# A planner's clock for TensorE that counts changes of the used part of the array

## The reference, cut to what matters

```python
def first_block(x, p, ...):
    for l in range(DEPTH):
        mix = even_mixer(...) if l % 2 == 0 else odd_mixer(...)
        x = layer_norm(ALPHA * x + mix, ln1_g[l], ln1_b[l])
        hdn = jnp.square(jax.nn.relu(x @ ffn_w1[l]))
        x = layer_norm(ALPHA * x + hdn @ ffn_w2[l], ln2_g[l], ln2_b[l])
        e = rms_norm(p[l] @ ple_w_proj[l], ple_norm_g[l])
        x = x + jax.nn.sigmoid(x @ ple_w_gate[l]) * e
    return x
```

## Time and profile before

| | |
|---|---|
| median of 3 runs | 1855.76 us (1855.68 to 1857.1) |
| profiled execution, span from first to last instruction | 1854.1 us |
| PE busy | 1788.8 us, 96% |
| DVE busy | 1275.2 us, 69% |
| ACT busy | 990.7 us, 53% |
| mean granted clock of PE | 0.989 |

### The profile page before, as it was taken

One profiled execution on the slowest core, in us unless ns is written; L12 is line 12 of the kernel. 1 busy time (PEld: TensorE's weight loads), 2 busy tenths in 40 slices (PEclk: granted clock), 3 DMA queues, 4 the chain that ended last, 5 costly groups with the idle time before them and its releaser, 6 DMA issues. The chain is left out here.

```text
span 1854.1 us, 35690 instructions
## 1 busy us (share of the span) xinstructions
PE 1788.8 (96%) x14792; PEld 1663.2 (90%) x14792; DVE 1275.2 (69%) x2351; ACT 990.7 (53%) x1741; POOL 76.2 (4%) x78
## 2 busy tenths in 40 slices
PE   7999999999999999999889999999999999989997
PEld 6778899978888999999889988899999898679997
DVE  5566656568778755886766777765676867876665
ACT  4565545466556544654755655554455555644443
POOL 0000100020000200000100101000000000100000
PEclk9999999999999999999999999999999999989999
DMA  9797865676344555455454443455655543236663
GB/s 377 273 354 253 325 184 190 185 291 195 122 117 140 165 185 185 126 171 182 128 174 155 149 159 93 150 178 184 186 177 193 162 137 107 86 114 185 184 186 120
DMA packets 93825, 334.92 MB, mean 181 GB/s; under 512 B 10960, under 2 KB 12880, under 8 KB 93536
## 3 DMA queue, kind: packets, MB, share of 16 engines
q1 hardware_dynamic: 92016, 327.33, 54.1%
q0 software_dynamic: 1648, 5.31, 0.9%
HBM read 331.55 MB, written 1.05 MB: 179 GB/s over the span
## 5 line engine op out<-in xcount | busy, mean ns | idle before, releaser
L565 DVE TENSOR_TENSOR low<-ring,high 128x1024 fp32r<-128x1024 f32 x410 | 500.8, 1223 | 218.4 <-ACT high L557 209.0
L590 PE MATMUL bank<-XHx,high 128*128 128x256 f32 x2096 | 608.7, 290 | 21.9 <-DVE low L565 9.7
L591 PE MATMUL bank<-XLx,high 128*128 128x256 f32 x2096 | 592.2, 283 | 0.0
L592 PE MATMUL bank<-XHx,low 128*128 128x256 f32 x2096 | 591.0, 282 | 0.0
L557 ACT CAST high<-ring 128x1024 fp32r<-128x1024 f32 x410 | 428.6, 1045 | 276.0 <-PE bank L592 230.5
L590 PEld LDWEIGHTS bank<-XHx,high 128*128 128x128 f32 x2096 | 397.6, 190 | 41.3 <-issue 9.7
L591 PEld LDWEIGHTS bank<-XLx,high 128*128 128x128 f32 x2096 | 398.1, 190 | 1.5 <-issue 0.2
L592 PEld LDWEIGHTS bank<-XHx,low 128*128 128x128 f32 x2096 | 398.2, 190 | 0.0
L590 PE MATMUL bank<-XHc,high_side 128*128 128x256 f32 x608 | 180.9, 297 | 10.2 <-DVE low_side L565 8.1
L591 PE MATMUL bank<-XLc,high_side 128*128 128x256 f32 x608 | 172.0, 283 | 0.0
L592 PE MATMUL bank<-XHc,low_side 128*128 128x256 f32 x608 | 171.7, 282 | 0.0
(11 more groups left out here) (448 smaller groups left out, 3052.1 us busy)
## 6 DMA issues: line engine op xcount, KB each, us to landing
ring<-in_stream SPq DMA_DIRECT2D x410, 512.0 KB, 3.7
ring_side<-in_stream SPq DMA_DIRECT2D x110, 512.0 KB, 3.7
ring_mod<-in_stream SPq DMA_DIRECT2D x96, 512.0 KB, 8.0
x_nb<-in_rpb POOLq DMA_DIRECT2D x6, 256.0 KB, 3.1
x_late_NB<-in_rpb POOLq DMA_DIRECT2D x6, 256.0 KB, 3.1
Xx<-in_x SPq DMA_DIRECT2D x2, 512.0 KB, 5.8
Xc<-in_ctx SPq DMA_DIRECT2D x1, 1024.0 KB, 7.0
out<-y SPq DMA_DIRECT2D x8, 128.0 KB, 2.0
```

The source lines that it names most:

```text
L565: nc.vector.tensor_tensor(st.low[:, j % st.n_ring, :], st.ring[:, j % st.n_ring, :], st.high[:, j % st.n_split, :].bitcast(F32), ALU.subtr ...
L590: nc.tensor.matmul(out, wh, xh, start=(i == 0), stop=False)
L591: nc.tensor.matmul(out, wh, xl, start=False, stop=False)
L592: m = nc.tensor.matmul(out, wl, xh, start=False, stop=(c == ks[-1]))
```

## The change

TensorE's lane remembers which part of the array was used last (`rows_cols`). Every place that emits matmuls now first calls `T.shape(rows, cols)`, which adds 0.2 us to the clock when the part differs from the last one. A full product's pass is charged n / 2180 us, other matmuls n x passes / 2370 without the 0.006. The 64x64 pieces of GLA are charged 0.03 us, its state steps three passes instead of four, and the 0.45 us for each run of modulation tiles is dropped. Nothing else is changed: no instruction is added or removed, and the plans and ranks stay.

```diff
@@ class Lane
+        self.rows_cols = P, P
...
+    def shape(self, rows, cols):
+        if (rows, cols) != self.rows_cols:
+            self.clock += SHAPE_US
+            self.rows_cols = rows, cols
...
 def T_us(n, passes=1):
-    return max(n * passes / 2270.0, 0.06) + 0.006
+    return max(n * passes / 2370.0, 0.06)
+
+
+def pass_us(n):
+    return n / 2180.0
+
+
+SHAPE_US, QUARTER_US = 0.2, 0.03
...
@@ def products (and rows_product, in the same way)
+            T.shape(P, P)
...
-                m.then_inc(*T.tick(k.s_products, 3 * T_us(n), key, *used))
+                m.then_inc(*T.tick(k.s_products, 3 * pass_us(n), key, *used))
...
-                T.spend(3 * T_us(n))
+                T.spend(3 * pass_us(n))
...
@@ def tensor_modulations
+                T.shape(P, 32)
...
-                if c % MOD_BATCH == 0:
-                    T.spend(0.45)
...
+            T.shape(P, P)
...
@@ def tensor_scores
+            T.shape(HD, P)
...
@@ def tensor_values
+                T.shape(P, P // len(one))
...
@@ def tensor_gla
+        T.shape(32, P)
...
+            T.shape(HD, CH)
...
-                        T.spend(T_us(CH, 2))
+                        T.spend(QUARTER_US)
...
+            T.shape(CH, P)
...
-                *T.tick(k.s_states, T_us(P, 4), (tag(i), "step", n)))
+                *T.tick(k.s_states, T_us(P, 3), (tag(i), "step", n)))
...
+            T.shape(HD, HD)
...
-                T.spend(T_us(CH, 2))
+                T.spend(QUARTER_US)
```

More of the change, by code:

```diff
@@ L593, in products @@
             if c == ks[-1]:
-                m.then_inc(*T.tick(k.s_products, 3 * T_us(n), key, *used))
+                m.then_inc(*T.tick(k.s_products, 3 * pass_us(n), key, *used))
             elif used:
-                m.then_inc(*T.tick(st.s_used, 3 * T_us(n), *used))
+                m.then_inc(*T.tick(st.s_used, 3 * pass_us(n), *used))
             else:
-                T.spend(3 * T_us(n))
+                T.spend(3 * pass_us(n))
             yield None
@@ L633, in rows_product @@
             if c == DC - 1:
[L634 removed]
+                m.then_inc(*T.tick(k.s_products, 3 * pass_us(n), keys[i], *mine))
             elif mine:
[L636 removed]
+                m.then_inc(*T.tick(st.s_used, 3 * pass_us(n), *mine))
             else:
[L638 removed]
+                T.spend(3 * pass_us(n))
             yield None
@@ L1597, in tensor_hgrn @@
     k.bank_of[tag, "inner"] = b0
+    T.shape(P, CH)
     for i in range(2 * NQ):
@@ L1842, in tensor_gla @@
                     if c == CHUNKS - 1:
-                        m.then_inc(*T.tick(k.s_mixers, T_us(CH, 2), (tag(i), "inner scores", hh)))
+                        m.then_inc(*T.tick(k.s_mixers, QUARTER_US, (tag(i), "inner scores", hh)))
                     else:
-                        T.spend(T_us(CH, 2))
+                        T.spend(QUARTER_US)
             yield None
@@ L1869, in tensor_gla @@
         halves = [slice(hh * HD, (hh + 1) * HD) for hh in range(2)]
+        T.shape(P, HD)
         for tile in range(NQ):
```

## The result

| | before | changed |
|---|---|---|
| median | 1856.43 us (1855.68 to 1858.21) | 1867.22 us (1865.39 to 1868.23) |
| ratio, 95% interval | | 1.0065 [1.0049, 1.0081] |
| span of the profiled execution | 1854.1 us | 1866.9 us |

The account below looks back on a forecast made before the run. TensorE, busy 1788.8 of 1854.1 us, was taken as the bound, so order could move only idle time, lower-clock time and shape changes. 1855.8 - 5.6, all else nil, gave 1850.2 us; range 1839 to 1866.

Parts of the forecast that it names:

- The sum of the clock: TensorE's planner clock, order unchanged: -14.4 - 10.8 - 23.5 + 64.6 = +15.9 us over the kernel, about +4 by 902 us.
- the tie at 902: Layer norm near 902 us: the side tile's low part goes before the norm's steps on DVE, -5.6 us (uncertain from 0).
- The second term: All other reordered choices across the kernel: gains and losses cancel, taken as nil; change count bounded at 6.4 us either way.
- The slower rival: Side tiles due earlier cause a new PE wait during a norm: 8.8 us more, 1864.6 us; chance 0.24.
- the two-tile ring: Side tile buffer: each tile needs 8.0 us from the freeing of its place, so PE may wait during a norm.
- earlier due times: Side stream's plan, 840 to 1300 us: 0.5 tile more asked for at 902, 1.5 to 2 at the stretch's end.
- the prediction's own signs of being wrong: Whole kernel: a wait over 3 us at a new place, lower-clock stretches growing, or change count moving over a tenth.
- The other signs: Near 900 us: wait 2 us or less, no lower clock; around 960: wait 4 to 5 us; 1000 to 1300: side one to two tiles ahead.
- The ring's chain: Side tile at 962.88 us: load at 954.91 to PE's start takes 8.0 us, little shortened by rank; gain taken as 0.
- the rule about draining: Changing the tiling mode drains TensorE; each change is paid whether booked or not, so booking alone would gain nil.

Follow-up runs that it names:

- the two tried orders: Changed kernel with small moves of its charge, lag and plan constants, two sets chosen by replaying the orders: 1846.60 us (0.9951) and 1849.36 us (0.9964).
- side plan +1: Changed kernel with every time of the side stream's plan 1 us later (481, 841, 1301, 1531): 1857.61 us, ratio 1.0015 to the kernel before.

## Why the prediction was wrong

The sum of the clock held. The order moved almost everywhere, the number of changes of shape was 318 (323 before, forecast 290 to 355), and the single charges are what the rows show. PE's busy time rose by 7.0, at the very edge of the 7 us allowed; 5.7 of that is the lower clock.

The step that failed is the one from there to a time, in both of its terms. The first is the tie at 902, put at -5.6. It did not turn: the norm moved by 18 us, another side tile met it, and its low part came 4.4 us after its cast, as in the old order. PE's wait for a side tile (5.4 us) is gone there, but one of 4.3 us for the gate's first product stands at the same norm, with 6.8 us at the lower clock from 922.2 on. The second term is everything else, put at nothing ("the reshuffled ties gain here what they lose there"). With the first term at nothing, the second measured +10.8: new waits of PE and the clock after them, 5.8 and 5.7 us by the two profiles. A saving at one place of a list schedule can't be forecast with the rest of the order held fixed, since the order after it is another.

Is the second term zero in the mean? Of the nine kernels above in which charges or the plan were moved without trial (all but the two tried orders), eight are slower than the kernel before, by 0.15 to 1.2%, and one equals it. Six of the nine are the changed kernel and its neighbours, so they are no even sample. But none of them is faster: the kernel before is low in the spread, though not the lowest, as the tried orders show, and a move from it is likely up. Nothing in its profile says so directly, but the size of what the order can move was there to read: 65.3 us not busy and 20.4 at the lower clock, less the start and the norms.

The range failed by the same step. Its upper end allowed one new wait of 5.4 us with its echo in the clock (8.8 us, 1864.6, and 1.4 around it). There came seven of 1.9 to 4.7 us for the three that went, and the time was 1.2 us above the range. The slower rival had the sign, and its mechanism, the two-tile ring while a norm runs, made one of the seven waits (1492 us; 7.9 us from load to use, forecast 8.0). The wait of 3.1 at 1218 is for a side tile too; the other five are of other kinds. Its reason, earlier due times, is not borne out: with the side stream two tiles later the kernel is slower still, and with the plan 1 us later it is nearly back. Two of the prediction's own signs of being wrong were met: waits over 3 us stand at 925, 1218 and 1492, where there was none, and the stretches at the lower clock grew.

The other signs: the wait for a side tile in the c_hidden products around 960 was to stay at 4 to 5 us and is gone. The ring's chain is there, from a load at 956.91 to a low part that begins at 961.69, but PE has other work meanwhile; so another order can cover such a chain, which the prediction priced at no gain. No stretch at the lower clock was forecast at the norm; there is one from 922.2 to 929.0. And side tiles were to be ahead by one to two between 1000 and 1300 us: at equal time they are ahead by none to one.

On the rule about draining (the Trainium skill, "TensorEngine Tiling (Array Packing)", Key Properties): the trace agrees in kind, with 0.39 us for two changes. By it booking the changes brought nothing in itself; that is nearer to the result than the forecast, but the slower time has another cause, the order. That a change of shape costs about 0.2 us is as sure as the earlier trace rows make it; that booking it helps the planner is what no run here shows.

## What to carry to other kernels

When estimates only decide an order, do not expect a better estimate to give a better order: here a change of 0.1% in one constant cost about 5 us, and 1 us in the plan gave 10 back. Judge such a change over several neighbouring constants, not by one pair of kernels, and if the order matters, try many and keep the best (here 0.5% below the kernel before). To forecast one, take the time the engine is not busy plus what the lower clock takes as the amount that can move, and ask whether the present order is already low in it.

## What the runs showed of the hardware

The granted clock fell to 1.2 GHz after short waits too: after 2.5 us at 1598 (0.51 for 3.4 us), and after 1.3 us in the kernel before at 1197.8. The length of a single wait does not tell it. In the kernel before the clock fell at 1482.5 though no wait in the 8 us before was over 1.1 us, and it stayed at full through one of 1.55 us at 1608.6:

```profile
1482.50:1485.90 3.40, 3.40 (x14) 3.11 (x13) 3.40 (x10) 2.60 (x5) 0.00 (x0) 0.50 0.01 5
1606.50:1613.00 6.50, 4.95 (x37) 3.18 (x34) 5.96 (x16) 2.82 (x7) 2.88 (x3) 1.00 0.14 43
```

In "side plan +1" it stayed at full through a wait of 2.36 us at 1481.2. Over the twelve kernels the lower clock costs 16.6 to 30.0 us, 0.28 to 0.39 us for each us in which PE is not busy, which makes each new wait dearer than it looks in the list.
